# One layer's pooling as banded matmuls, gate units in another bank, and square roots ahead of the norms' sums, in a four-layer hybrid trunk

## What is computed

```python
def multiscale_pool(h, buf, start_pos, w_grp, scale):
    hp = jnp.concatenate([buf.astype(h.dtype), h], axis=1)
    cs = jnp.pad(jnp.cumsum(hp.astype(F32), axis=1), ((0, 0), (1, 0), (0, 0)))
    pos = start_pos + jnp.arange(t)
    outs = []
    for gi, win in enumerate(POOL_WINDOWS):            # 2, 4, 8, 16, 256 channels each
        ...
        cnt = jnp.minimum(pos + 1, win).astype(F32)[None, :, None]
        outs.append((hi - lo) / cnt)
    pooled = jnp.concatenate(outs, axis=-1).astype(h.dtype) - h
    y = jnp.einsum('btgc,gcd->btgd', pooled, w_grp).reshape(bsz, t, D_MODEL) * scale
    return y, hp[:, t:]
```

## Time and profile before

| | |
|---|---|
| median of 3 runs | 1710.97 us |
| the profiled execution, its own time | 1707.89 us |
| its span on the engines | 1705.8 us |
| PE busy | 1564.0 us (92%) |
| POOL, DVE, ACT busy | 1000.9, 862.1, 671.9 us |
| bytes moved | 212.35 MB, 124 GB/s |

### The profile page before, as it was taken

The page is one execution under the profiler, slowest core; times in us unless marked ns, Lnnn a source line. Parts: engine busy times, 40 slices in busy tenths (PEclk is TensorE's granted clock), DMA queues, the critical chain, the costliest instruction groups (busy, mean ns, idle before and its releaser), DMA issues.

```text
span 1705.8 us, 32389 instructions
## 1 busy us (share of the span) xinstructions
PE 1564.0 (92%) x10261; PEld 1504.5 (88%) x10261; DVE 862.1 (51%) x1947; ACT 671.9 (39%) x1211; POOL 1000.9 (59%) x893
## 2 busy tenths in 40 slices
PE   6999999955999998998999997987988978999997
PEld 5999999945999997877999997986887877999997
DVE  3355553157555216785555412757758674555502
ACT  5555443324444344226544434541213122544432
POOL 5557777724777776534777675643242233777674
PEclk9999999977999999999999999989888998999999
DMA  5334445513444654212555455331303122444453
GB/s 193 124 117 160 148 148 153 152 45 111 160 149 152 161 155 125 70 54 79 158 157 154 134 141 163 124 94 62 134 1 132 45 95 94 161 148 148 124 146 110
DMA packets 87731, 212.35 MB, mean 124 GB/s; under 512 B 25488, under 2 KB 33200, under 8 KB 87536
## 3 DMA queue, kind: packets, MB, share of 16 engines
q1 hardware_dynamic: 87664, 211.49, 39.9%
HBM read 201.80 MB, written 9.66 MB: 124 GB/s over the span
## 4 chain that ended last, share of the span: by engine, by line
PE 85%; DVE 7%; issue 5%; ACT 2%; DMA 1%; POOL 0%; DVEq 0%; SPq 0%; POOLq 0%; ACTq 0%
PE bank L632 24%; PE bank L634 24%; PE bank L633 24%; PE bank L785 3%; PE bank L907 1%; PE bank L915 1%; PE bank L918 1%; PE bank L943 1%; DVE M L1558 1%; PE bank L832 0%; DVE ssq L1364 0%; DMA raw<-in_a_in 0%; DVE Hl_spare L1853 0%; DMA fst<-in_d_st 0%; PE bank L827 0%
## 5 line engine op out<-in xcount | busy, mean ns | idle before, releaser
L522 POOL TENSOR_TENSOR wlo<-raw,whi 128x512 fp32r<-128x512 f32 (+3 forms) x404 | 461.6, 1143 | 478.3 <-ACT whi L1003 435.4
L632 PE MATMUL bank<-Gh,whi 128*128 128x320 f32 x1928 | 606.7, 315 | 32.6 <-DVE Gl L1356 20.8
L634 PE MATMUL bank<-Gh,wlo 128*128 128x320 f32 x1928 | 598.8, 311 | 0.0
L633 PE MATMUL bank<-Gl,whi 128*128 128x320 f32 x1928 | 598.7, 311 | 0.0
L524 POOL TENSOR_TENSOR wlo<-raw,whi 128x512 fp32r<-128x512 f32 (+2 forms) x404 | 478.3, 1184 | 0.0
L632 PEld LDWEIGHTS bank<-Gh,whi 128*128 128x128 f32 x1928 | 364.8, 189 | 39.1 <-issue 29.6
L1003 ACT ACTIVATE whi<-raw 128x1024 fp32r<-128x1024 f32 (+3 forms) x404 | 374.1, 946 | 44.6 <-PE bank L634 36.2
L633 PEld LDWEIGHTS bank<-Gl,whi 128*128 128x128 f32 x1928 | 365.0, 189 | 1.5
L634 PEld LDWEIGHTS bank<-Gh,wlo 128*128 128x128 f32 x1928 | 364.7, 189 | 0.0
L632 PE MATMUL bank<-Hh,whi 128*128 128x320 f32 x912 | 287.2, 315 | 46.3 <-DVE Hl L1349 23.7
L633 PE MATMUL bank<-Hl,whi 128*128 128x320 f32 x912 | 284.6, 312 | 0.0
(11 more groups left out here) (278 smaller groups left out, 1772.5 us busy)
## 6 DMA issues: line engine op xcount, KB each, us to landing
raw<-in_f_up SPq DMA_DIRECT2D x176, 512.0 KB, 3.3
raw<-in_f_down SPq DMA_DIRECT2D x64, 384.0 KB, 3.2
raw<-in_f_down SPq DMA_DIRECT2D x64, 320.0 KB, 3.2
raw<-in_c_pw SPq DMA_DIRECT2D x24, 512.0 KB, 3.6
raw<-in_a_in SPq DMA_DIRECT2D x16, 512.0 KB, 3.7
raw<-in_d_qk SPq DMA_DIRECT2D x16, 512.0 KB, 3.6
raw<-in_d_vg SPq DMA_DIRECT2D x16, 512.0 KB, 8.1
raw<-in_a_out SPq DMA_DIRECT2D x8, 512.0 KB, 3.6
```

Of the source, the lines that this page charges most:

```text
L522: pool.tensor_tensor(wlo[k][:, 0:half], raw[k][:, 0:half], whi[k][:, 0:half].bitcast(F32), ALU.subtract).then_inc(half_ready, 1)
L632: nc.tensor.matmul(dst, wh, h, start=start and n == 0, stop=False)
L633: nc.tensor.matmul(dst, wh, lo, start=False, stop=False)
L634: ins = nc.tensor.matmul(dst, wl, h, start=False, stop=stop and n == len(tiles) - 1)
```

## The change

Pooling. The part is laid out as matmuls. ACT writes the gained X of norm 2 as plain fp32 into `Gf`, which lies over Gh, and DVE makes no Gl for it. PE transposes each tile of Gf behind the down tiles of layer 0 (`turn_x`) and the pool state once (`turn_pool_state`); ACT copies both out. POOL builds four bands (1/w on w diagonals, minus the identity) in layer 0's up phase. PE sums the squares a second time by columns, so that tokens lie on the partitions, ACT and DVE make the factor column of it, and DVE scales the rows of the bands with it. Five matmuls a tile (`pool_tile`) then give the pooled tile, ahead of the `b_grp` units and two tiles early. The new pool state is made on POOL (`pool_states`) with R. Layer 0's down phase is written out in place of a loop on PE and ACT, and layer 0's up phase on POOL.

Gates. `d_ab` goes into `acc[3]`; `d_qk` units 0 to 2 no longer wait for its eviction; the turn comes after unit 1, and PE's wait for POOL's clearing moves there.

Roots. `std` takes a root of a constant column before it waits; the last norm's sum takes seven squares from DVE and the eighth from ACT directly.

```diff
+        Gf = nc.alloc_sbuf_tensor_at("Gf", [P, KT * NT], F32, offset=nc.sbuf_base - 4 * KT * NT)
...
                     if l == 1:
-                        sp.wait_ge(unit_done, START["f_up", 1] + 1)
+                        sp.wait_ge(pool_state, 3)
                         sp.dma_start(out["pool"], pnew).then_inc(stored, 16)
...
+            def pooling_bands(g):
+                w, B = POOLW[g], band[g]
...
+                G.mark(pool.memset(B[:, 16:BW], 1.0 / w))
+                G.mark(pool.tensor_copy(B[:, 0:16], par[:, COL["inv"] + 16 * g:COL["inv"] + 16 * g + 16]))
+                G.wait()
+                G.mark(pool.affine_select(out=x, in_=x, compare_op=ALU.is_ge, fill=0.0, base=0,
+                                          pattern=[[1, P + 16]], channel_multiplier=-1))
...
+                pool.tensor_tensor(x[:, 0:P], x[:, 0:P], ident[:, :], ALU.subtract).then_inc(band_ready, 1)
+                pool.tensor_tensor(y, y, ident[:, :], ALU.subtract).then_inc(band_ready, 1)
+                G.wait()
+                pool.tensor_tensor(n, n, ident[0:64, 0:64], ALU.subtract).then_inc(band_ready, 1)
+            def pool_states():
+                pool.wait_ge(r_ready, 1)
+                pool.wait_ge(pool_in, 16)
+                pool.wait_ge(g_hi, KT * 3)
...
+                for b in range(NB):
+                    ins = pool.tensor_tensor(new[:, :, 22 + 15 * b:30 + 15 * b], x[:, :, SEQ + DEC * b:SEQ + DEC * (b + 1)],
...
+                ins.then_inc(pool_state, 1)
+                for b in range(NB):
+                    ins = pool.tensor_copy(new[:, :, 15 + 15 * b:22 + 15 * b], old[:, :, b, 8:15])
+                ins.then_inc(pool_state, 1)
...
+                if name == "f_up" and l == 0:
+                    for b in range(n // 4):
+                        for k in range(4):
+                            split_lo(b * 4 + u0 + k, k, w)
+                        if b in (2, 4, 6, 8):
+                            pooling_bands(b // 2 - 1)
+                    continue
+                if name == "b_grp":
+                    for k in range(4):
+                        if k == 2:
+                            pool_states()
+                        split_lo(u0 + k, k, w)
+                    first = 1
...
+                if l == 0:
+                    for m in range(2, KT):
+                        out_tile(u0 + 4 * m, m % 2, u0 + 4 * (m - 1))
+                        if m == KT - 2:
+                            turn_pool_state()
+                        turn_x(m - 2)
+                    return
...
+            def column_sums():
+                pe.wait_ge(ssq_ready, KT * 3)
+                nc.tensor.matmul(mixb[2][:, 0:1], ssq[:, 0:128], ones[:, 0:1], start=True, stop=True)
...
+            def pool_tile(m):
...
+                pe.wait_ge(band_scaled, 3 * (g + 1))
+                if m >= 2:
+                    pe.wait_ge(h_ready, htile(1, False) + m - 1)
+                nc.tensor.matmul(dst[:, 128:256], xT[m][:, 128:256], B[:, BAND1:BANDN], start=True, stop=False)
+                nc.tensor.matmul(dst[:, 128:144], xT[m][:, 0:128], B[:, 128:144], start=False, stop=True)
+                nc.tensor.matmul(dst[:, 0:128], xT[m][:, 0:128], B[:, 0:128], start=True, stop=True)
+                nc.tensor.matmul(dst[:, 256:320], px, C[0:120, BANDO:BW], start=True, stop=False)
+                nc.tensor.matmul(dst[:, 256:320], xT[m][0:64, 256:384], B[0:64, BANDN:BANDO], start=False, stop=True)\
+                    .then_inc(h_mid, 1)
...
+                turn_x(KT - 2)
+                column_sums()
+                turn_x(KT - 1)
                 norm_stat(2)
...
+                pool_tile(0)
+                pool_tile(1)
+                for m in range(KT):
+                    if m + 2 < KT:
+                        pool_tile(m + 2)
+                    pe.wait_ge(evac, u0 + m - 2)
+                    unit(u0 + m, m % 4, Hh, Hl, acc[m % 4][:, 0:NT], (m // 2 * 2, m // 2 * 2 + 1),
+                         ready=(h_ready, htile(1, False)))
...
-                pe.wait_ge(evac, u0)
+                pe.wait_ge(evac, u0 - 4)
...
-                pe.wait_ge(consts, ZEROS)
...
-                    in_unit(u0 + k, k)
-                    if k == 0:
+                    pe.wait_ge(evac, u0 - 4 if k < 3 else u0)
+                    unit(u0 + k, k, Gh, Gl, acc[k][:, 0:NT], range(KT))
+                    if k == 1:
+                        pe.wait_ge(consts, ZEROS)
                         pe.wait_ge(ab_v, G_READY)
...
-            norm_stat(NORMS)
+            pe.wait_ge(ssq_ready, KT * NORMS + KT - 1)
+            nc.tensor.matmul(stat[:, 0:NT], ones[:, :], ssq[:, :], start=True, stop=False)
+            pe.wait_ge(sq_ready, KT * (NORMS + 1))
+            nc.tensor.matmul(stat[:, 0:NT], ones[:, :], sq[1][:, 0:NT], start=False, stop=True).then_inc(stat_done, 1)
...
             def std(done, value, ready):
+                nc.scalar.activation(spare1[:, 0:1], eps[:, 0:1], ACT.Sqrt)
                 act.wait_ge(done, value)
...
+            def x_columns(m):
+                act.wait_ge(x_turned, m + 1)
+                nc.scalar.activation(xT[m][:, 0:256], mixb[m % 2][:, 0:256], ACT.Copy)
+                nc.scalar.activation(xT[m][0:64, 256:384], mixb[m % 2][0:64, 256:384], ACT.Copy).then_inc(xT_ready, 1)
...
+                x_columns(KT - 2)
+                act.wait_ge(colsum_done, 1)
+                nc.scalar.activation(rcol[:, 0:2], mixb[2][:, 0:2], ACT.Sqrt, scale=1.0 / D, bias=eps[:, 0:1])
...
+                x_columns(KT - 1)
                 std(stat_done, 3, std_ready)
...
+                pooled_hi(0)
+                pooled_hi(1)
+                act.wait_ge(pool_state, 2)
                 for m in range(KT):
+                    if m + 2 < KT:
+                        pooled_hi(m + 2)
+                    ahead(u0, 0, m, 0)
+                    residual(3, m, m % 2, evac, u0 + m + 1)
...
+                dve.wait_ge(colstd_ready, 1)
+                S.mark(vec.reciprocal(rcol[:, 0:2], rcol[:, 0:2]))
...
+                    vec.tensor_scalar(C[:, BAND0:BAND1], B[:, BAND0:BAND1], rcol[:, 0:1], None, ALU.mult).then_inc(band_scaled, 1)
+                    vec.tensor_scalar(C[:, BAND1:BANDN], B[:, BAND1:BANDN], rcol[:, 1:2], None, ALU.mult).then_inc(band_scaled, 1)
...
+                dve.wait_ge(std_ready, 3)
+                vec.reciprocal(R[:, :], sd[:, :]).then_inc(r_ready, 1)
...
+                pooled_lo(0)
+                pooled_lo(1)
                 for m in range(KT):
...
+                    if m + 2 < KT:
+                        pooled_lo(m + 2)
+                    dve.wait_ge(unit_done, u0 + m + 1)
+                    vec.scalar_tensor_tensor(out=x, in0=acc[m % 4][:, 0:NT], scalar=col("b_scale", m), in1=x,
+                                             op0=ALU.mult, op1=ALU.add).then_inc(evac, 1)
+                    residual(3, m, m % 2, m == 0)
```

More of the change, by code:

```diff
@@ L571, in _ @@
+            G = Steps(pool, band_steps)
             for name, l, n, w in phases:
@@ L606, in _ @@
                         pool.memset(ap, 0.0).then_inc(consts, 1)
-                if name == "f_up" and l in (0, 1) and l + 1 < layers:
-                    pool.wait_ge(stored, 16 * (l + 1))
-                    if l == 0:
-                        for i in range(2):
-                            pool.memset(hp[i][:, 0:15], 0.0).then_inc(consts, 1)
-                    else:
+                if name == "f_up" and l == 1 and l + 1 < layers:
+                    pool.wait_ge(stored, 32)
+                    if True:
                         pool.memset(zpad.rearrange("p (m c) -> p m c", c=CW)[:, :, 0:30], 0.0).then_inc(consts, 1)
@@ L772, in glu_units @@
                             pe.wait_ge(z_ready, m)
-                        unit(u, u % 4, Gh, Gl, acc[v][:, 0:NT], range(KT), ready=(g_ready, KT * 4) if m + v == 0 else None)
+                        unit(u, u % 4, Gh, Gl, acc[v][:, 0:NT], range(KT), ready=(g_ready, gains(4)) if m + v == 0 else None)
                         if m + v == 0:
@@ L1033, in residual @@
                 separate(m)
-                if e < NORMS:
+                if e == 2:
+                    nc.scalar.activation(tile_of(Gf, m), tile_of(X, m), ACT.Copy,
+                                         scale=col("gain", m + e * KT)).then_inc(g_hi, 1)
+                elif e < NORMS:
                     nc.scalar.activation(tile_of(Gh, m), tile_of(X, m), ACT.Copy,
@@ L1091, in ffn @@
                 down_body(l, 0)
+                if l == 0:
+                    for b in range(1, 4):
+                        down_body(l, b)
+                    nc.scalar.activation(rcol[:, 3:4], eps[:, 0:1], ACT.Sqrt)
+                    return
                 with act.Fori(1, 3) as b:
@@ L1352, in residual @@
             def residual(e, m, i, first):
-                if e < NORMS:
+                if e < NORMS and e != 2:
                     dve.wait_ge(g_hi, m + (e * KT + 1))
@@ L1440, in ffn @@
```

(17 more changed lines are left out.)

144 lines of the change are left out of this document (97 added, 47 removed).

## The result

The changed kernel takes 1691.8 us, the median of four executions (1686.1 to 1695.7), where the kernel before, run beside it, takes 1710.4. The ratio is 0.9889, with a 95% interval of 0.9858 to 0.9919. A second round of five executions gave 1692.1 and 0.9905 (0.9892 to 0.9919). The prediction was 1690.5, in a range of 1684.5 to 1699.0: faster as forecast, 1.3 us above the number. But the agreement is in part luck: it hides two errors of opposite sign, and most of what follows is about them.

A forecast was written before the change was run, and what follows sets the result against it. TensorE, holding 85% of the chain, was taken as the bound, time being gained where it stands still. Terms: 20.4 - 2.2 - 0 + 2.3 + 0 = 20.5 us, from 1710.97 to 1690.5 us; range 1684.5 to 1699.

The forecast's parts named there:

- the stage: Layer 1's pooling, X of layer 0's last down tile to first up unit: 51.45 to 31.05 us, gain 20.4.
- transposes in layer 0's down phase: 23 added PE transposes before the last down tile's end cost 2.2 us, bounds 2.2 and 3.5.
- bands: POOL's four band-building bursts in layer 0's up phase, 4.8 us each, are hidden and cost 0.
- gates: Layer 3's gate units in the fourth bank: unit 2 starts earlier, worth 2.3 us, bounds 0 and 2.7.
- roots, last sum: Constant root before each norm's wait and last sum by PE: 0 us, the table load already being ahead.
- its two idle places: PE stands still in layer 1's mixer (51.45 us place) and behind layer 3's gate units (waits 7.56 and 3.31 us).
- The head: Pooling stage's start, s being X of layer 0's last down tile: R at s+8.8, X of tile 0 about s+13.0.
- rival 3: Pooling head stays late as ACT, DVE and POOL hang on one another: X0 at s+18, 1695.5 us; chance 0.14.
- The steps: Pooling stage, X to X: first 3.2 us, four at 2.65, one without new tiles at 2.02.
- rival 1: Half clock in the new pooling stage: PE's 3.6 to 3.8 us make the step, some 5 us, 1696; chance 0.16.
- the cover of 6.3 us: Layer 0's up phase: POOL's 1.96 us idle plus 4.3 lead let a burst of up to 6.3 us cost nothing.
- Rival 2: POOL's band bursts stall layer 0's up phase: at 10.1 us each, loss 15.2, time 1706; chance 0.10, 0.04 slower than before.

The follow-up runs named there:

- seven traces: Two traces of the changed kernel and five of follow-ups that leave the stage's code as it is; the stage takes 31.4 to 36.9 us, mean 33.8.
- the two pairs: Gate part taken back: in the changed kernel, 1692.95 us against 1692.1; in the kernel with three idle PE stretches of the pooling stage filled, 1689.8 against 1688.0.
- the clock held: Changed kernel with unread matmuls in three idle PE stretches of the pooling stage, two in its head and one between pool tiles 1 and 2: 1688.0 us, 0.9869.
- the fillings: Changed kernel with ten unread matmuls in each of PE's two idle stretches in the pooling stage's head: 1687.15 us, 0.9868.
- the two heavier kernels: Changed kernel with POOL building its bands twice in each burst, 1700.5 us (0.9946), and three times, 1722.8 us (1.0068).

## Why the prediction was right, and where it was wrong

| term | predicted, us (bounds) | measured, us |
|---|---|---|
| the stage | 20.4 (15.7 to 23.2) | 17.7 (14.6 to 20.1 in seven traces) |
| transposes in layer 0's down phase | -2.2 (-2.2 to -3.5) | -2.4 |
| bands | 0 | 0 |
| gates | 2.3 (0 to 2.7) | 1.7 by traces; 0.8 by medians and 0.9 by ratios in the two pairs |
| roots, last sum | 0 (-0.3 to 0.4) | 0.0 |
| sum | 20.5 | 17.0; the medians differ by 18.6 |

There is one trace of the kernel before, so the stage and the gates stand against one draw of a clock that varies, and that execution (1707.89) was itself 2.5 us below the median beside it. Between the stage and layer 3, and behind it, the code is the same in both, and the distances scatter by 1 to 2 us from trace to trace, which is the size of the 1.6 left over. The lower bound of the stage, 15.7, was not low enough: the first trace has 14.6.

**The bound and the places.** Right: PE bounds the kernel, and filling its two idle places brought the gain.

**The head.** R at s+8.9, as worked out (8.8). The band scaling took 2.3 us (2.1 was booked), `pool_states` 0.44 + 2.26 = 2.7 (2.7), its copies 1.45 (some 2). X of tile 0 was put at s+13.0; with the clock held it is at s+12.5, and without at s+14.2 to 14.8. So the chain through ACT, DVE and POOL was right, and rival 3 (s+18) did not occur. The miss is PE: a pool tile was priced at 1.1 us from the earlier trace rows and takes 1.29 at full clock and 2.5 at the lower level, and three of them with a unit behind make 9.1 us from 365.1 on.

**The steps.** This is the step that failed. 2.65 was booked from DVE's and ACT's extra operations. At full clock they are 2.44, 0.4 over the 2.05 of before: DVE's Hl comes on top (0.40 us from its start to the next one's), ACT's Hh fits into ACT's idle time. At the lower level they are 4.11, and that level is not the exception but comes in each of the seven traces, for 10.2 to 23.9 us. The argument against rival 1, that PE works 75% of a step, was the wrong question: PE was busy 100% and the clock stayed low all the same. With the clock held the stage takes 28.8 us, 2.25 less than the 31.05 forecast; as it runs it takes 33.8 on the mean, 5.0 more than that. The rival's price (some 5 us) was right, its chance (0.16) was not, and the forecast came out near because head and steps together had been sized 2.25 us too large. That is luck; so is that the kernel before ran at 1710.4 beside the changed one and not at the 1711.0 from which the 20.5 had been taken. The Trainium skill (TensorE: Matmul & The Clock Gate, "Why this matters for your kernels") advises against idle gaps above a certain length between matmul bursts; the fillings bear out the direction, but the gaps here, 1.48 and 1.41 us, are shorter than the ones it names. That a busy PE gets the higher level back soon, which the Trainium skill suggests (same page, Part 1), does not hold for the stretches above.

**The transposes.** X of the last down tile comes only 1.78 us later than before, but layer 0's up phase began 0.65 us earlier in that trace (X of the last mixer tile at 124.46 in place of 125.11). From that X to X of the last down tile are 232.98 us before and 235.41 in each trace of the changed code, so 2.4 us, within the bounds: 23 transposes at 0.106, a little over the 0.095 of the earlier trace rows. PE has no gap in the phase, as forecast.

**The bands.** 0 as booked, 4.1 us for 4.8. And the cover of 6.3 us, put together from 1.96 idle and 4.3 lead, was confirmed to 0.1 us by the waits of the two heavier kernels. Rival 2 was a true one: three times the work is slower than the kernel before. What it lacked was the clock behind the waits.

**The gates.** The positions were right: unit 0 waits for POOL, the turn for G1, which stays at 21.8 us behind X (21.6 before; up to 22.5 in other traces), and unit 2 starts 23.25 us behind X, where 22.98 was worked out. The lower bound had named the likely reason for the shortfall: the two new gaps hold the clock low behind each, and cost about 1.1 of 2.8 us, by one trace with the gaps filled. The expected second wait "near as long as the first" was 2.05 (3.7 in the second trace) against 4.95.

**The roots.** Right: the load was ahead of the wait already. The constant root even delays the real one by 0.1 us (1037.29 and 1037.40, behind a load that ended at 1037.28).

## What to carry to other kernels

When serial vector work moves onto a TensorE that stood still, price the new stage at the lower clock first, and ask of the stretch ahead of it, not of the stage, whether the clock will be up. The low clock behind idle stretches of 1.4 to 1.5 us cost 5 us of the stage here, and 20 matmuls that nobody reads made the kernel 5.0 us faster. For a burst on a helper engine, idle time plus lead makes the cover, and it was worked out here from one timeline to a tenth of a microsecond; what the clock adds behind a wait comes on top. One trace on each side is too little for terms of 1 to 3 us: take the same distance in every trace at hand, and between two instructions that enclose only the code that was changed. Distances from the start of the span carry what came before: they put the transposes at 1.8 us in place of 2.4.

## What was not expected of the hardware

A TensorE that the profile shows busy without a gap ran at 0.50 from 365 to 388.8 us, with the same instructions that ran at 1.00 from the start where the head had been filled. What ends such a spell stays open: in seven traces it lasted from 10.2 to 23.9 us. Nor does the length of an idle stretch alone decide whether the clock falls. Of four stretches of 2.0 us, each alone in a busy phase, two were followed by 3.4 us at 0.50 and two were not. All four of 6.1 us were. And in two of the seven traces of the stage the one stretch of 1.48 us lay ahead of the fall, while in the other five the second one had begun.

Small operations of POOL are cheap: a product of 64 columns in eight strided runs 0.28 us, a select of 64 to 144 columns 0.28 to 0.31, a copy of 56 columns 0.18.
